# The last norm: reciprocal roots of four row tiles on GpSimd, one tile at a time

## The reference

```python
def ln_affine(x, g, b):
    xf = x.astype(jnp.float32)
    mu = jnp.mean(xf, -1, keepdims=True)
    var = jnp.mean(jnp.square(xf - mu), -1, keepdims=True)
    y = (xf - mu) * lax.rsqrt(var + LN_EPS) * g.astype(jnp.float32) + b.astype(jnp.float32)
    return y.astype(x.dtype)

# in trunk_layer, applied to context and latent tokens:
    y = hier_moe(h, p['w_coarse'][l], p['b_coarse'][l], p['w_fine'][l], p['b_fine'][l],
                 p['w_gate_up'][l], p['w_down'][l])
    x = ln_affine(DEEPNORM_ALPHA * x + g2 * y, p['ln2_g'][l], p['ln2_b'][l])
```

## Time and profile before

| what | us |
| --- | --- |
| runs, median (lowest to highest of 3) | 1321.29 (1317.66 to 1322.39) |
| the profiled execution | 1319.52 |
| its span, first to last instruction | 1317.6 |
| busy in the span: PE | 1233.5 (94%) |
| busy: DVE | 947.3 (72%) |
| busy: ACT | 655.6 (50%) |
| busy: POOL | 231.8 (18%) |

### The profile page before, as it was taken

The page is one execution under the profiler, slowest core; times in us unless marked ns, Lnnn a source line. Parts: engine busy times, 40 slices in busy tenths (PEclk is TensorE's granted clock), DMA queues, the critical chain, the costliest instruction groups (busy, mean ns, idle before and its releaser), DMA issues.

```text
span 1317.6 us, 20528 instructions
## 1 busy us (share of the span) xinstructions
PE 1233.5 (94%) x6711; PEld 1006.8 (76%) x6711; DVE 947.3 (72%) x1714; ACT 655.6 (50%) x1043; POOL 231.8 (18%) x347
## 2 busy tenths in 40 slices
PE   7999999999999899998998999993899999999994
PEld 4677777778888799887876788783788888888862
DVE  5665531848461789888877524788999999999957
ACT  1522222232222688776773212224488878888843
POOL 0024441021242000011111000101111211222111
PEclk9999999999999999998998999995899999999998
DMA  9888995472655476542004543637999999999955
GB/s 349 280 298 274 289 293 218 163 236 86 223 161 215 164 226 225 182 140 81 25 24 121 182 140 98 210 148 262 335 379 366 370 390 389 388 385 375 378 199 129
DMA packets 152834, 309.44 MB, mean 235 GB/s; under 512 B 20700, under 2 KB 31516, under 8 KB 152760
## 3 DMA queue, kind: packets, MB, share of 16 engines
q1 hardware_dynamic: 122456, 233.24, 49.7%
q0 software_dynamic: 24384, 70.00, 17.3%
q10 hardware_dynamic: 5920, 5.24, 1.3%
HBM read 259.24 MB, written 61.24 MB: 243 GB/s over the span
## 4 chain that ended last, share of the span: by engine, by line
PE 81%; DVE 11%; issue 3%; DMA 2%; ACT 2%; SPq 1%; POOL 0%; DVEq 0%; ACTq 0%; POOLq 0%
PE psum_pair L1805 9%; PE psum_pair L1807 8%; PE psum_pair L1806 8%; PE psum_pair L1905 6%; PE psum_pair L2089 5%; PE psum_pair L2091 5%; PE psum_pair L2090 5%; PE psum_pair L1916 4%; PE psum_pair L1972 4%; PE psum_pair L1974 4%; PE psum_pair L1973 4%; PE psum_pair L1931 3%; PE psum_pair L2104 3%; PE psum_pair L2106 3%; PE psum_pair L2105 3%
## 5 line engine op out<-in xcount | busy, mean ns | idle before, releaser
L1805 PE MATMUL psum_pair<-w_parts,h_hi 128*128 128x512 f32 x520 | 206.3, 397 | 3.0 <-DVE h_lo L1313 3.0
L1807 PE MATMUL psum_pair<-w_parts,h_lo 128*128 128x512 f32 x520 | 203.6, 391 | 0.0
L1806 PE MATMUL psum_pair<-w_parts,h_hi 128*128 128x512 f32 x520 | 203.3, 391 | 0.0
L1164 DVE TENSOR_TENSOR w_parts<-w_raw,w_parts 128x1024 fp32r<-128x1024 f32 x72 | 83.3, 1220 | 97.4 <-ACT w_parts L878 96.9
L1018 ACT ACTIVATE p_unnormed<-psum_pair,minus_max 128x640 f32<-128x640 f32 (+1 forms) x160 | 113.4, 711 | 59.2 <-DVE minus_max L1391 59.0
L1391 DVE TENSOR_REDUCE minus_max<-psum_pair 128x1 f32<-128x640 f32 (+1 forms) x160 | 111.7, 715 | 22.7 <-PE psum_pair L1905 20.6
L1905 PE MATMUL psum_pair<-k_bundle,q_bundle 128*128 128x320 f32 (+1 forms) x576 | 115.7, 326 | 12.2 <-ACT p_unnormed L1018 10.8
L1805 PEld LDWEIGHTS psum_pair<-w_parts,h_hi 128*128 128x128 f32 x520 | 98.1, 189 | 25.1 <-issue 5.6
L1807 PEld LDWEIGHTS psum_pair<-w_parts,h_lo 128*128 128x128 f32 x520 | 98.0, 189 | 21.0
L1806 PEld LDWEIGHTS psum_pair<-w_parts,h_hi 128*128 128x128 f32 x520 | 98.0, 189 | 19.6
L1905 PEld LDWEIGHTS psum_pair<-k_bundle,q_bundle 128*128 128x128 f32 x576 | 86.2, 190 | 27.2 <-issue 24.8
(11 more groups left out here) (361 smaller groups left out, 2646.8 us busy)
## 6 DMA issues: line engine op xcount, KB each, us to landing
w_raw<-in_w_gate_up SPq DMA_DIRECT2D x76, 512.0 KB
w_raw_c<-in_w_gate_up SPq DMA_DIRECT2D x72, 512.0 KB
w_raw_b<-in_w_down SPq DMA_DIRECT2D x72, 512.0 KB, 8.8
w_raw<-in_w_in SPq DMA_DIRECT2D x52, 512.0 KB
ada_raw<-in_w_ada SPq DMA_DIRECT2D x32, 512.0 KB, 9.3
k_transposed<-turned_staging POOLq DMA_DIRECT2D x48, 256.0 KB, 7.4
k_bundle<-k_transposed SPq DMA_DIRECT2D x14, 768.0 KB, 7.9
q_transposed<-turned_staging POOLq DMA_DIRECT2D x40, 256.0 KB, 6.4
```

The source lines that it names most:

```text
L1164: dve.tensor_tensor(w_parts[b % 2][:, 1, c], w_raw[:, c], w_parts[b % 2][:, 0, c].bitcast(F32), ALU.subtract).then_inc(lo_done, 1)
L1805: pe.matmul(out, a_hi, hi, start=kk == 0, stop=False)
L1806: pe.matmul(out, a_hi, lo, start=False, stop=False)
L1807: return pe.matmul(out, a_lo, hi, start=False, stop=kk == KD - 1)
```

## The change

The roots of tiles 0 to 3 move from VectorE to GpSimd, one root for each tile. GpSimd has other instructions at hand, so its root is 11 TENSOR_SCALARs on one column; the halving of the bits is folded into a multiplication by −0.5. Every one of them increments `gp_step` and the next waits for it. The semaphore `words_set`, which had been counted to 4 by four IOTAs earlier, is renamed to `gp_step` and counted on. VectorE keeps the root of tile 4. A root no longer waits for the square of the second tile of a pair, and ScalarE's squares and scalings alternate. The stores stay on GpSimd, between the roots.

```diff
             def norm_z(tt):
-                act.wait_ge(zr_done, tt // 2 + 1)
+                act.wait_ge(zr_done, tt + 1)
                 act.wait_ge(zg_done, tt + 1)
                 act.activation(ya[:, tt], yc[:, tt], ACT.Copy, scale=zr[:, tt:tt + 1]).then_inc(zn_done, 1)
 
             square_z(0)
             square_z(1)
             norm_z(0)
+            square_z(2)
             norm_z(1)
-            square_z(2)
             square_z(3)
             norm_z(2)
+            square_z(4)
             norm_z(3)
-            square_z(4)
...
             combine(1)
             gain_z(1)
-            root_z(slice(0, 2))
             combine(2)
             gain_z(2)
             combine(3)
             gain_z(3)
-            root_z(slice(2, 4))
             combine(4)
             gain_z(4)
-            root_z(slice(4, 5))
+            root_z(4)
             finish_z(4)
...
             pool.wait_ge(out_cleared, 16 * TL)
-            for tt in range(TL):
+            steps = [4]
+
+            def step(ins):
+                steps[0] += 1
+                ins.then_inc(gp_step, 1)
+                pool.wait_ge(gp_step, steps[0])
+
+            def root_z(tt):
+                y, v, half = zr[:, tt:tt + 1], zv[:, tt:tt + 1], zt[:, 1:2]
+                pool.wait_ge(zq_done, tt + 1)
+                step(pool.tensor_scalar(v, zq[:, tt:tt + 1], 1.0 / D, EPS, ALU.mult, ALU.add))
+                step(pool.tensor_scalar(y.bitcast(I32), v.bitcast(I32), -0.5, float(RSQRT_MAGIC), ALU.mult, ALU.add))
+                for _ in range(3):
+                    step(pool.tensor_scalar(half, y, y, v, ALU.mult, ALU.mult))
+                    step(pool.tensor_scalar(half, half, -0.5, 1.5, ALU.mult, ALU.add))
+                    step(pool.tensor_scalar(y, y, half, None, ALU.mult))
+                pool.nop().then_inc(zr_done, 1)
+
+            def store_z(tt):
                 dst = t["y_sample"][0, tt * P:(tt + 1) * P]
                 pool.wait_ge(zn_done, tt + 1)
                 pool.dma_start(dst, ya[:, tt], accum_op=ALU.add).then_inc(out_st, 16)
+
+            root_z(0)
+            root_z(1)
+            store_z(0)
+            root_z(2)
+            store_z(1)
+            root_z(3)
+            store_z(2)
+            store_z(3)
```

More of the change, by code:

```diff
@@ L599, in hybrid_step @@
         route_done = sem("route_done")
-        words_set = sem("pair_words_set")
+        gp_step = sem("pair_gp_step")
         picks_done = sem("slot_picks_done")
@@ L1523, in take_logits @@
                                               ALU.mult, ALU.add))
-            dve.wait_ge(words_set, 4)
+            dve.wait_ge(gp_step, 4)
             link(dve.tensor_scalar(words[:, :, :, 0:2], words[:, :, :, 0:2].bitcast(U32), -1.0, float(NOBODY), ALU.mult, ALU.add))
@@ L1721, in combine @@
                 dve.wait_ge(z_done, tt + 1)
-            def root_z(c):
-                n = c.stop - c.start
-                dve.wait_ge(zq_done, c.stop)
+            def root_z(tt):
+                c = slice(tt, tt + 1)
+                dve.wait_ge(zq_done, tt + 1)
                 link(dve.tensor_scalar(zv[:, c], zq[:, c], 1.0 / D, EPS, ALU.mult, ALU.add))
[L1727 to L1732, removed]
+                rsqrt_column(dve, link, zr[:, c], zv[:, c], zt[:, 0:1], zi[:, 0:1])
             def gain_z(tt):
@@ L2275, in _ @@
                 if v == 0:
[L2276 to L2279, removed]
+                    pool.iota(words[:, :, :, 0].bitcast(U32), [[NT * P, 2], [P, NT]], base=0, channel_multiplier=1).then_inc(gp_step, 1)
+                    pool.iota(words[:, :, :, 1].bitcast(U32), [[0, 2], [P, NT]], base=0, channel_multiplier=1).then_inc(gp_step, 1)
+                    pool.iota(places[:].bitcast(U32), [[1, P]], base=0, channel_multiplier=0).then_inc(gp_step, 1)
+                    pool.iota(table[:], [[0, TCOLS], [0, 4]], base=NOBODY, channel_multiplier=0).then_inc(gp_step, 1)
             pool.wait_ge(mg_done, 4 * NT)
@@ L2352, in _, with root_z @@
             pool.nop().then_inc(pool_turn, 1)
-            pool.wait_ge(out_cleared, 16 * TL)
-            for tt in range(TL):
+            steps = [4]
[3 more added lines that the diff above has]
+                pool.wait_ge(gp_step, steps[0])
+            def root_z(tt):
+                y, v, half = zr[:, tt:tt + 1], zv[:, tt:tt + 1], zt[:, 1:2]
[8 more added lines that the diff above has]
+            def store_z(tt):
                 dst = t["y_sample"][0, tt * P:(tt + 1) * P]
@@ L2358, in _ @@
                 pool.dma_start(dst, ya[:, tt], accum_op=ALU.add).then_inc(out_st, 16)
+            pool.wait_ge(out_cleared, 16 * TL)
+            root_z(0)
[6 more added lines that the diff above has]
+            store_z(3)
             for s in range(2):
```

## The result

The changed kernel took 1327.57 us, median of 6 runs (1326.53 to 1331.39), the kernel before 1321.17 (6 runs): ratio 1.0054, interval 1.0038 to 1.0070, so 0.5% slower. Measured again later (e6) with 6 more runs against 29 of the kernel before, the ratio was 1.0073 (1.0048 to 1.0098). The profiled execution has a span of 1325.0 us, where 1325.3 was forecast.

The account below looks back on a forecast made before the run. VectorE was taken to bound the last stretch, in a program bound by TensorE. The walk through GpSimd's shut-out roots gave span 1325.3 against 1317.6, +7.7; 1321.29 + 7.7 = 1329.0 us, range 1319 to 1340.

Parts of the forecast that it names:

- VectorE freed, TensorE next: Last stretch: two roots leave VectorE, 5.06 us; TensorE's pace leaves 3.82, tile 4 starting at 1300.34 in place of 1304.16.
- Shut out beside L1719 and the gain: GpSimd's small instructions stand still while VectorE reads two SBUF tensors, leaving six steps a tile where a root has 11.
- The step: One GpSimd root instruction takes 0.36 us: 0.19 busy plus 0.17 wake-up, within 0.22 to 0.98.
- The walk: GpSimd's four roots traced through the openings, ready at 1294.3, 1301.65, 1307.9 and 1314.1; last store issued at 1315.4.
- The squares behind scalings: On ScalarE square 4 queues behind scaling 2, so VectorE idles 6 us before its root; prompt 2.2 us later.
- The sum, +7.7: Whole program: span 1325.3 against 1317.6 us, so 7.7 us slower.
- two terms of the landing: End of the kernel: the last store of a close pair lands 7.1 us after issue; the span ends 2.73 us later.
- The span ends 2.73 us after the later landing: End of the kernel: the prompt's store lands last, at 1314.87, and the span ends at 1317.6.
- The chances: Whole time: slower by over 0.5% (above 1327.9 us) 0.54, within it 0.43, faster by more 0.03.
- The rivals: Alternatives for GpSimd's roots: port open (0.22), short steps with port shut (0.11, +2 to +5), long steps (0.14, +14 to +32).
- an open port: L1719 and L1735 do not shut GpSimd out; a root takes 4.0 us, span 1316.6, −1.0 us; chance 0.22.
- two ways out at the end: End of the kernel: the prompt's store lands at 1314.87, the last sample store at 1313.67, 1.2 us apart.

Follow-up runs that it names:

- e6: The changed kernel, unchanged, measured and profiled once more with more runs: ratio 1.0073 to the kernel before, median 1332.00 us.
- e2: Changed kernel with L1719 and the gain each reading one operand from PSUM in place of SBUF, leaving residual and gate out: 1322.96 us, ratio 1.0013.
- e9: Changed kernel with L1717 writing its product back to PSUM and L1719 reading it there, nothing left out: ratio 1.0056 to the kernel before.
- e8: Changed kernel with roots 2 and 3 back on VectorE as a pair, L1719 reading its product from PSUM, square 4 last: ratio 0.9991 to before.
- e3: Changed kernel with ScalarE's squares moved ahead, so none stands behind a scaling that waits for the previous tile's root: ratio 1.0066 to the kernel before.
- e1: The kernel before, unchanged, profiled once more: ratio 0.9988, stage length 34.50 us.
- e7: Changed kernel with L1719 reading its product from PSUM and two Newton steps in place of three in GpSimd's roots: ratio 0.9976 to the kernel before.
- e5: Kernel before with only ScalarE's order of squares and scalings changed to the alternating one, roots staying in pairs on VectorE: ratio 1.0010.

## Why the prediction was right, point by point

- **VectorE freed, TensorE next**: right. Tile 4 starts at 17.34 from the stage's start, as forecast (1300.34 − 1283.00).
- **Shut out beside L1719 and the gain**: right, and shown by e2, where the operand's place differs, and for L1719 by e9, which leaves nothing out. In the changed kernel's profile alone it would still be an inference from end times. That the second to issue is the one that is blocked fits most of the long steps, but not all: in e9 and e8 a step that the profile has starting 0.05 and 0.07 us before a gain (1285.04 against 1285.09 in e9) was held to the gain's end too, while VectorE was not. And the longest case of the earlier trace rows, a COPY that got no turn between back-to-back L1649s, is not the rule: the COPY of the earlier trace rows at 933.39 ended at 934.40, 0.05 behind the first of three L1649s that ran on to 936.62.
- **The step**: 0.36 forecast, 0.35 measured, but made up otherwise. The wake-up behind GpSimd's own instruction is 0.08 to 0.10, not the 0.17 taken from waits for other engines; a step that reads column scalars is busy 0.28 (one) or 0.34 (two), not the 0.19 of a COPY. The errors cancel.
- **The walk**: roots were forecast ready 11.3, 18.65, 24.9 and 31.1 after the stage's start; they were ready at 9.8, 17.8, 24.4 and 30.8. Root 0 got one step more ahead of L1719 than counted, and so met two shut stretches in place of three; root 1 then started earlier and met four in place of three. The issue of the last store was forecast at 32.4 and measured at 32.32. The nearness is in part luck: root 3 was ready 0.3 earlier than forecast, and the hand-over to the last store was longer. Store 2 starts 0.58 behind GpSimd's last step and takes 0.9, and store 3 starts behind it, 0.29 after the end of scaling 3 and not 0.15.
- **The squares behind scalings**: VectorE idles 5.46 for a forecast 6, and its end is late, 30.0 for a forecast 30.6. In the sum it stood only through L1740 pushing root 3, and e3, which takes the late square away, does not shorten the stage (45.56).
- **The sum, +7.7**: the stage grew by 9.75. The forecast was 2.05 short, and two terms of the landing were too small. "The span ends 2.73 us after the later landing" rested on the prompt's store landing last, at 1314.87. In all 12 profiles the span ends 3.9 us behind the last *sample* store's landing (3.87 to 3.97, as landings are given to a tenth). In the kernel before and five others the prompt's store lands about 1.2 us after that, and both readings fit; in the changed kernel it lands far earlier, at 1313.3, and only the 3.93 behind the sample store fits. That is 1.2 us more than the 2.73. Whether the prompt's store alone could set the end was not tried. And the last store of a close pair takes 7.0 to 9.4 us to land, not 7.1: here 8.1, 1.0 us. The span agreed with the forecast only because this execution reached the stage 2.35 us earlier, which is scatter (e1, e6): luck.
- **The chances**: slower by over 0.5% had 0.54. The first ratio, 1.0054, lies barely beyond that, and its median, 1327.57, just under the 1327.9 named for it; the second ratio, 1.0073, lies well beyond. The forecast of 1329.0 missed the first median by 1.4 us and the second, 1332.00, by 3.
- **The rivals**: an open port comes to 36.75 (e2), still 2.2 us over before, where the rival said −1.0. It carried the same two terms of the landing (1.3 and 1.2 us), and the last store came 0.65 later than its 23.8, with stores that start 0.6 behind a root in place of 0.15. So even with both instructions opened the stage is longer than before the move.

## What to carry to other kernels

Before work is moved to GpSimd, look at what VectorE runs beside it: in these runs its small instructions stood still while VectorE read two tensors from SBUF, and a chain of small dependent steps pays that again and again. Work in openings, not in busy shares: a chain that fits between two shut stretches costs what its steps cost (e7: 2.66 us in an opening of 3.06), and one that is longer loses a stretch in every turn (e9: 3.86 us). If one operand of VectorE's instruction can lie in PSUM, the shut stretch is gone, and here VectorE's own times stayed as they were (L1719 in e9 and e7). And with two ways out at the end, find from a second kernel's profile which landing the end really follows.

## What the runs showed of the hardware

- A small GpSimd instruction that comes while VectorE is in an instruction with two SBUF tensors ends 0.04 to 0.22 us behind it (1.15 and 1.26 us for steps that otherwise take 0.34 and 0.19). A store that GpSimd issues is not held: the first one, beside L1719, takes 1.00 us in the changed kernel and 1.00 in e2, where L1719 reads one SBUF tensor. VectorE did not lose to GpSimd: its L1717, L1719 and gain kept their spacing of 1.25 to 1.27 and 1.45 to 1.47 us in all runs.
- L1717 takes 1.23 us whether it writes to SBUF or back to PSUM, and L1719 1.22 to 1.23 with its second operand in either (e7).
- GpSimd on one column of 128 partitions, with a semaphore between: 0.27 to 0.30 us from start to start with immediates alone, 0.38 with one column scalar, 0.42 with two. About 0.1 of each (0.08 to 0.10) lies between the end of one and the start of the next. VectorE's own root has 0.18 to 0.26 from start to start.
- An adding store of 512 KB issued by GpSimd lands after 5.0 to 6.1 us when no other is issued within 2 us, and the last one after 7.0 to 9.4 as the second of two about 1 us apart. What parts the 7.0 from the 9.4 was not looked into. In e5, where the last two are apart, the last took 5.3 us where it took 7.1 before.
